# A scan over eight head pairs: pair buffers cut from three to two

## The reference

```python
def step(S, inp):
    w_t, k_t, v_t, kk_t, a_t = inp[:5]
    sa = jnp.einsum('bhvk,bhk->bhv', S, -kk_t)
    S = (S * w_t[:, :, None, :] + sa[..., None] * (kk_t * a_t)[:, :, None, :]
         + v_t[..., None] * k_t[:, :, None, :])
    y = jnp.einsum('bhvk,bhk->bhv', S, inp[5]) if len(inp) == 6 else None
    return S, y
```

## Time and profile before

| | us |
|---|---|
| runs of the kernel (3) | 4030.27, 4044.8, 4056.88 |
| median | 4044.8 |
| profiled execution | 4030.27 |
| its span | 4028.9 |

### The profile page before, as it was taken

How to read it: one execution, slowest core, us unless ns; L and a number is a source line. 1 busy time by engine, 2 the same in 40 slices (tenths; PEclk the granted TensorE clock), 3 DMA queues, 4 the chain that set the end, 5 groups by cost and what they waited for, 6 DMA issues and landing times.

```text
span 4028.9 us, 72509 instructions
## 1 busy us (share of the span) xinstructions
PE 3655.5 (91%) x31840; PEld 2337.4 (58%) x31840; DVE 1652.8 (41%) x2928; ACT 1189.0 (30%) x2161; POOL 1362.1 (34%) x1214
## 2 busy tenths in 40 slices
PE   7998777999899989888899999899988888889998
PEld 3756565434444445555455555445676776748887
DVE  1244343134434121454524242653566656533344
ACT  3253222221212164443200000202556666420002
POOL 1320343011222021667433333434443434225444
PEclk9998678989998999999999999999999999989999
DMA  5430000520011211450111111132100000022222
GB/s 195 143 107 22 1 2 12 204 82 19 29 53 43 79 52 37 173 189 31 44 63 57 59 63 47 68 107 85 41 16 16 28 16 4 14 84 95 84 84 74
DMA packets 196419, 263.76 MB, mean 65 GB/s; under 512 B 6119, under 2 KB 151655, under 8 KB 194056
## 3 DMA queue, kind: packets, MB, share of 16 engines
q1 hardware_dynamic: 189168, 242.78, 18.2%
q10 hardware_dynamic: 6936, 16.35, 1.1%
HBM read 246.52 MB, written 12.58 MB: 64 GB/s over the span
## 4 chain that ended last, share of the span: by engine, by line
PE 74%; ACT 9%; DVE 6%; issue 5%; POOL 4%; DMA 1%; ACTq 0%; DVEq 0%; SPq 0%; POOLq 0%
PE ps L238 58%; PE ps L3026 3%; PE ps L763 2%; PE ps L381 1%; PE ps L488 1%; ACT mem L840 1%; PE ps L2023 1%; PE ps L790 1%; PE ps L778 1%; DVE mem L1223 1%; PE ps L497 1%; ACT mem L2961 1%; ACT mem L665 1%; DVE mem L821 1%; POOL mem L2929 1%
## 5 line engine op out<-in xcount | busy, mean ns | idle before, releaser
L238 PE MATMUL ps<-mem 64*64 64x64 f32 (+4 forms) x25280 | 2696.6, 300 | 163.1 <-ACT mem L665 33.1
L238 PEld LDWEIGHTS ps<-mem 64*64 64x64 f32 (+1 forms) x25280 | 1753.3, 154 | 1115.9 <-issue 571.0
L2929 POOL TENSOR_TENSOR mem<-mem 128x256 f32<-128x256 f32 (+1 forms) x264 | 225.2, 865 | 348.4 <-ACT mem L3438 172.7
L858 POOL TENSOR_SCALAR mem<-mem 128x768 f32<-128x768 f32 (+2 forms) x128 | 219.0, 1723 | 193.3 <-DVE mem L824 193.3
L2205 ACT ACTIVATE mem<-ps 128x384 f32<-128x384 f32 (+1 forms) x80 | 35.5, 445 | 778.8 <-PE ps L238 736.5
L2192 POOL TENSOR_TENSOR mem<-mem 128x512 f32<-128x512 f32 (+1 forms) x80 | 100.1, 1251 | 445.2 <-PE ps L238 368.5
L595 POOL TENSOR_TENSOR mem<-mem 128x512 f32<-128x512 f32 (+1 forms) x72 | 75.2, 1061 | 427.3 <-ACT mem L590 424.2
L2216 DVE TENSOR_TENSOR mem<-mem,ps 128x384 f32<-128x384 f32 (+1 forms) x80 | 39.9, 499 | 414.5 <-PE ps L238 414.5
L3026 PE MATMUL ps<-mem 128*128 128x128 f32 x960 | 175.9, 301 | 31.3 <-DVE mem L2951 20.1
L2959 ACT ACTIVATE mem<-ps 128x256 f32<-128x256 f32 (+1 forms) x220 | 101.5, 461 | 195.3 <-PE ps L3026 195.1
L2951 DVE TENSOR_TENSOR mem<-mem,ps 128x256 f32<-128x256 f32 (+1 forms) x220 | 109.7, 514 | 117.4 <-PE ps L238 116.7
(11 more groups left out here) (329 smaller groups left out, 4120.1 us busy)
## 6 DMA issues: line engine op xcount, KB each, us to landing
mem<-i_mod_w SPq DMA_DIRECT2D x48, 1024.0 KB, 6.8
mem<-i_ffn_wg SPq DMA_DIRECT2D x22, 1024.0 KB, 5.4
mem<-i_ffn_wu SPq DMA_DIRECT2D x22, 1024.0 KB, 5.3
mem<-i_e_w_in SPq DMA_DIRECT2D x16, 1024.0 KB, 6.1
mem<-i_o_w_in SPq DMA_DIRECT2D x16, 1024.0 KB, 5.7
mem<-i_ffn_wd SPq DMA_DIRECT2D x16, 1024.0 KB, 5.2
mem<-i_e_mod_w SPq DMA_DIRECT2D x12, 1024.0 KB, 10.8
mem<-i_o_mod_w SPq DMA_DIRECT2D x12, 1024.0 KB, 6.5
```

The source lines that it names most:

```text
L238: ins = e.h.matmul(out, l, r, start=(i == 0), stop=(i == n - 1))
L858: K.pool.h.tensor_scalar(w, w, stat(i, o, 1), None, MUL).then_inc(*nm.up(tag, i, o))
L2929: K.pool.h.tensor_tensor(m3(self.slot(l)), self.lraw, bm(C(K, f"cm{self.d}", l, 64), 2 * self.np), MUL).then_inc(*self.mk.up(key, l))
```

## The change

The third buffer and its semaphore are taken away. Pair `hp` uses buffer `hp % 2`, and the loads of pairs 2 to 7 wait for `fi_out` of pair `hp - 2`. Buffer 1 stays the one in the weight ring's memory.

```diff
@@ Scan.__init__
-        self.bufs = [ec(BUF), w[:, NSLOT * SLOT - BUF:], K.alloc(BUF)]
+        self.bufs = [ec(BUF), w[:, NSLOT * SLOT - BUF:]]
...
-        self.ld = [K.sig(f"ld_pair{i}") for i in range(3)]
+        self.ld = [K.sig("ld_pair0"), K.sig("ld_pair1")]
@@ Scan.loads
         for hp in range(1, 8):
-            if hp >= 3:
-                K.sp.wait_ge(*self.out.at(hp - 3))
-            b, s = self.bufs[hp % 3], self.ld[hp % 3]
+            if hp >= 2:
+                K.sp.wait_ge(*self.out.at(hp - 2))
+            b, s = self.bufs[hp % 2], self.ld[hp % 2]
             K.sp.h.dma_start(b[:, 0:384], K.ins["hpw"][hp]).then_inc(*s.up(hp, 0, by=16))
             K.sp.h.dma_start(b[:, 384:2432], K.rkv[hp]).then_inc(*s.up(hp, by=16))
 
     def loaded(self, hp):
-        return self.ld[hp % 3].at(hp)
+        return self.ld[hp % 2].at(hp)
 
     def part(self, hp):
 
-        b = self.bufs[hp % 3]
+        b = self.bufs[hp % 2]
```

## The result

The changed kernel takes 4072.6 us (median of 9 runs, 4064.6 to 4083.5), the one before 4048.8 (9 runs, 4030.3 to 4056.9). The ratio is 1.0063, with a 95% interval of 1.0049 to 1.0078: slower by 25 us (the medians differ by 23.7), within 1% of before. Forecast were 4064.0, in a range of 4042 to 4087.

A forecast was written before the change was run, and what follows sets the result against it. The kernel was taken as bound by a chain between engines, not transfers or VectorE time. Six stalls of 3.2 us, 19.2 in all, on the median of 4044.8 gave 4064.0 us, in a range of 4042 to 4087.

The forecast's parts named there:

- The third buffer costs nothing: End of the allocation: removing 2432 columns moves later addresses and takes away no instruction; cost 0.
- the load of pair 1: Start of the pair loop: this load goes alone, with some 8 us of cover before its reader; gain or cost 0.
- Six late loads, and their issue and need: Pairs 2 to 7: each load waits for L3628, its reader wanting it 1.70 us after issue; six stalls.
- The landing, 5.2 us: Large load of each pair: lands 5.2 us after issue, so its reader L3270 starts 3.6 us late.
- 3.2 us of it pass on: VectorE's L3488 behind L3270: 3.2 us of each stall reach TensorE's in-order queue, between bounds 2.7 and 3.6.
- VectorE's rest of 0.42: VectorE before the first L3488: its 0.42 us rest for ScalarE's copy was to go, easing the delay.
- the 19.2 of the sum: Pair loop: six stalls of 3.2 us each add up to 19.2 us.
- C, the clock: TensorE behind each stall: idle gap lowers its clock, making the kernel over 1% slower; 0.06 beyond its 40.4 us point.
- the 6 us set aside for six dips of 1.0 us: Pair loop: small clock falls priced at 1.0 us each, 4070 in all, allowed for in the range.
- The large form of C: TensorE behind each stall: low clock for 10 us costs 7.0 us more a pair, 61 us in all, 4106.
- B, absorption: Pair loop: TensorE's rests take up the stall, leaving 4044.8, or 4054 if half; chance 0.09.
- D: Pair loads: the large load lands before its reader though asked for late, nothing lost; needs under 1.6 us; ruled out.

The follow-up runs named there:

- e1: Kernel before, three buffers kept, but loads of pairs 2 to 7 wait for the finish of pair hp - 2: 1.0064 of before.
- e5: Changed kernel's two buffers, each part loaded after its own last reader, keys and decay weights a period early: 1.0004 of before.
- e4: Changed kernel with each pair's load split, the keys loaded first under their own semaphore: 1.0014 of before, 6 us over.
- e6: Changed kernel with one more 1 MB transfer issued and waited for ahead of each load of pairs 2 to 7: 1.0141 of before.
- e9: Changed kernel with three unread TensorE products ahead of the claim of PSUM banks, so they run within each gap: 1.0036 of before.
- e10: Kernel before with three unread TensorE products ahead of the claim of PSUM banks, where there is no gap: 1.0051 of before.
- e2: Kernel before, three buffers, with the late wait for the loads of pairs 2, 4 and 6 only: 1.0023 of before.
- e11_before_again: Kernel before, unchanged, profiled a second time: a run of 4053.4 us.
- e3: Changed kernel with three unread TensorE products ahead of the wait for L3488, which ran behind the gap: 1.0089 of before.
- e7: Changed kernel with the front held back for 18 steps instead of 16: 1.0081 of before.
- e8: Kernel before, three buffers and early loads, with the front held back for 18 steps instead of 16: 1.0077 of before.

## Why the prediction was right, point by point

*The third buffer costs nothing, the load of pair 1 neither.* Right: e1, with three buffers, is as slow as the change, and e5, with two, took the time of before (1.0004, at most 0.2% more). From L3270 of pair 1 to the first L3628 it took 84.1 us, before 83.9.

*Six late loads, and their issue and need.* Right. SyncE's six waits, the issue 0.40 us behind each L3628's end, and the wait of L3270 for the transfer came as written.

*The landing, 5.2 us.* Too small in the profiled execution. The six landings were 4.9, 6.0, 6.2, 5.0, 4.9 and 6.7, on average 5.6, and L3270 came 3.9 us late on average instead of 3.6. I had set 4.8 to 6.0 as bounds; two of six lay above. The pattern stood in the trace of before: the load issued at 3036.09, on which the forecast is worked out, itself landed after 5.6 us, and the next after 6.0. The slowest, the sixth, is issued at a place where the kernel before issues none.

*3.2 us of it pass on.* Right in mechanism. L3488 came 0.49 us sooner behind L3270, where the forecast had VectorE's rest of 0.42 go, and TensorE's queue moved by all that was left, 20.6 us in six, against the 19.2 of the sum. TensorE's gaps for L3488, 21.3 us, agree with it. Across e4, the changed kernel and e6 the loss grows with the wait: 9.7, 23.1 and 49.3 us of it, and 6, 25 and 57 us lost, clock term included.

*C, the clock.* This is the term that the forecast's sum left out. I had priced a small dip at 1.0 us and set it into the range, not into the 4064.0. It measured 7.1 us in the changed kernel, four falls in six gaps at 1.5 to 2.4 us each, and e9 and e10 show that the gap brings it: with work in the gap there was no fall. The sum with it is 20.6 + 7.1 = 27.7 by profile, and 25 as timed. That the 6 us set aside for six dips of 1.0 us come near the 7.1 is luck: there were fewer falls, and each cost more. The growth of a period was 4.7 us on average, between the 3.2 forecast and the 5 that I had named as the sign of C. The large form of C, 7.0 us a pair, fell: even behind e6's gaps of 8 us the low level lasted for the 96 records and part of L3165, 1.6 to 2.6 us more a pair.

The rule that I had set beside C (the Trainium skill, TensorE: Matmul & The Clock Gate, Why this matters for your kernels), that an idle gap between bursts brings the lower clock back, is borne out here, though not in each pair: six falls in six gaps of 7.5 to 8.2 us, four in six gaps of 2.8 to 4.6.

*B, absorption.* Fell. e2's stalls stood one pair apart and were not taken up between. TensorE's rests did not shrink. From L3270 of pair 1 to that of pair 7 its waits for L2961 were 18.1 us in 42 times before and 18.1 in 42 in the changed kernel.

*D.* Fell at once, with the first wait.

## What to carry to other kernels

A buffer's number is not what counts, but the distance from its last reader to the first reader of what replaces it: with two instructions between them a load of 4.9 to 6.7 us shows with 3.1 to 4.9 us, and everything queued behind the waiting instruction is late with it, also what needs nothing from the load. Before paying for another buffer, look for the part that the early reader needs: loading it first left 6 of 25 us, and giving it back by its own last reader left none that could be measured. And price a new gap on TensorE above its length where the work behind it follows without a rest: here the clock added about a third to it in the changed kernel and a quarter in e6.

## What had not been expected of the hardware

Two of the six large DMA instructions kept SyncE for 1.48 and 1.86 us instead of 0.43, and these two loads were among the slow ones, landing after 6.0 and 6.7 us (in a row with the plain ones, SyncE's timeline):

```profile
2959.90 0.43 SPq L3138 DMA_DIRECT2D mem<-rkv  x1
...
3048.50 1.48 SPq L3138 DMA_DIRECT2D mem<-rkv  x1
...
3415.81 1.86 SPq L3138 DMA_DIRECT2D mem<-rkv  x1
```

In e5 issues at the same two places took 1.26 and 1.65 us. But a slow issue alone does not make a late landing. The load issued at 3141.7 took 0.43 us to issue and landed after 6.2. In e11_before_again the second lone load took 1.16 us to issue and landed after 5.6, as it did before with an issue of 0.43. The slow landings go by the place in the loop: in the changed kernel, before, e1, e3, e7, e8, e9, e10 and e11 the second and third loads behind an L3628 took 5.6 to 6.3 us, the first, fourth and fifth 4.8 to 5.4, but for one of 5.7 in e8. In e6, where each load follows a transfer of the same block, all six took 4.8 to 5.1. What makes them slow was not tried.

Whether a gap of some 3 us brings the clock down is not settled by its length. In the changed kernel gaps of 2.83 and 2.85 us brought no fall and one of 2.96 did; in e1 one of 2.89 did, and those of 2.87 and 3.09 did not. All the gaps of 3.2 us or more that stood unfilled in e1, e2, e6 and the changed kernel brought one. In e7 and e8, at another place in the pair, a fall stood behind gaps as short as 2.04 and 2.58 us.
